# A hybrid Fourier, retention and attention transformer on one core: channel products between projection pairs, a new order on ScalarE, and an output projection begun early

## The chip, the cores and the metric

The kernel runs on one core of a Trainium2 chip. The metric is device time in microseconds, the median of the runs of one program. Engines work in order, each on its own list of instructions, and wait for each other through semaphores: TensorE (PE; its weight loads are shown as PEld), VectorE (DVE), ScalarE (ACT), GpSimd (POOL) and SyncE (SP), which issues the DMAs.

## What is computed

Two layers act on 512 latent tokens and 256 context tokens of width 1024. Each layer is a half-step gated feed-forward network, a token mixing, and another feed-forward network; inputs of each are normalized and modulated by a vector computed from a condition. The token mixing is where the change lies (cut from the reference):

```python
def fourier_mix(u):
    g = u.reshape(b, l, FOURIER_GROUPS, FOURIER_GROUP_DIM)
    y = jnp.fft.fft2(g, axes=(1, 3), norm='ortho').real

# retention, per head, chunks of 128 tokens, in both directions
intra_decay = where(causal, exp(diff * log_gamma), 0)
q_decay, k_decay = exp((pos + 1) * log_gamma), exp((cl - 1 - pos) * log_gamma)
scores = einsum(qc, kc) * intra_decay
kv = einsum(kc, k_decay, vc)      # state = state * chunk_decay + kv
out = scores @ vc + (qc @ state) * q_decay

# attention, 8 heads on 2 key/value heads, window of 128 and the context
m = maximum(s_loc.max(-1), s_ctx.max(-1), sink)
denom = exp(s_loc - m).sum(-1) + exp(s_ctx - m).sum(-1) + exp(sink - m)
o = (p_loc / denom) @ v_window + (p_ctx / denom) @ v_ctx

out = concatenate([y_f, y_ret, y_att], -1) @ w_o
```

In the second layer the context tokens give keys, values and states only.

## The kernel before, in words

Activations stand transposed: 128 channels on the partitions, tokens along the free axis, 8 blocks of channels. A float32 product of weights and activations is made as three products of rounded parts (high by high, high by low, low by high). The work is a list of phases. In each, a "unit" is 128 output channels for all tokens, accumulated over 8 or 11 blocks in one of two PSUM tiles `pg[0]`, `pg[1]` (two banks each); units go in pairs. `unit` (line 710) waits for split weights (`s_w`) and for the PSUM tile to be read (`s_free`), and calls `split_product` (line 703). SyncE loads weights into `raw`; ScalarE rounds them to `whi` (`split_hi`, line 1117), VectorE subtracts to `wlo` (`split_lo`, line 1445). A unit's weights are split while the other unit of the pair is multiplied.

The token mixing has three parts.

**Input projection** (`win`), 16 tiles of 128 channels: 0 and 1 Fourier, 2 to 5 retention queries and keys, 6 and 7 values, 8 and 9 gates, 10 to 13 attention queries, 14 keys, 15 values. TensorE runs the first pair apart and the other seven in hardware loops over pairs. ScalarE copies each finished unit to `z` (line 1409), VectorE rotates the tiles of queries and keys (lines 1911 to 1914).

**Mixing** (`mix`; one per engine, order written out by hand). TensorE's list is: wait until the projection's PSUM tiles are read and rotated; channel products (line 853: for each block of 128 tokens, both Fourier tiles by a table of cosines and sines, into one of two halves `pa[0]`, `pa[1]` of a PSUM tile), which ScalarE (even blocks, line 1269) and VectorE (odd blocks, line 1748) scale and copy into `pq`; sequence products of `pq` with the table `dft_sb` (lines 866, 870) into `pn` and then `pg[0]`; transposes of values and keys for the retention (lines 881, 884); chunk states (line 905); retention turns, one per block and pair of heads: scores (line 918), decay by VectorE (line 1742), values and cross part (lines 931, 933); the variance of the output (line 943); attention. Meanwhile ScalarE loads the table of exponentials (line 1265), makes the key decays, state decays and query decays (lines 1272 to 1275) and the exponential of the decay table (line 1278), and copies retention queries (line 1232); VectorE makes the arguments of the decay table (lines 1685, 1689) and decays the queries (line 1697). Low parts of the Fourier output are made by VectorE inside the retention turns (`y_low`, line 1662), after turn 2 and after turn 4 or 5. GpSimd copies states to `cross` (line 645), subtracts for the low parts of attention keys `ak_lo` and queries `aq_st` (line 633), and from step to step of the attention runs its own small list.

**Attention** goes over units q (48 in layer 0, 32 in layer 1; one is a block of 128 queries of one head), two units a pair `pr`. PSUM tile `pg[q % 2]` holds the scores. For unit q: TensorE scores (lines 962 to 968); VectorE the maximum (line 1808) and its negation with the sink, `negm` (line 1816); ScalarE the exponential `prob` (line 1325), with the row sum `den`; TensorE transposes (line 1006); VectorE and ScalarE copy them (`probT`, lines 1801, 1337); per pair TensorE multiplies by the values (line 1023). Beside this runs the denominator of each pair: GpSimd `esink = negm + sink` (line 671), ScalarE its exponential (line 1315), GpSimd the sum (line 675), VectorE the reciprocal (line 1813), GpSimd the spreading (line 689), TensorE a transpose (line 1030), ScalarE a copy `rden_t` (line 1342), VectorE the product with the values `oatt` (line 1826), ScalarE its high part (line 1347) and GpSimd its low part `xlo` (line 633), which counts `s_y` up. GpSimd also makes the low part of the next head's queries behind the sum of two of the pairs. All engines issue in the order of their loops over q; in ScalarE's, the order inside a step is sink exponential, `prob`, copy of transposes, copy of reciprocals, high part, next queries.

**Output projection** (`wo`), 8 units of 8 blocks (0, 1 Fourier, 2, 3 retention, 4 to 7 one head of each key/value group): TensorE first waits until `s_y` has counted all low parts, then multiplies. It is the last phase of the mixing; the second feed-forward network follows.

## Time and profile before

| | before |
|---|---|
| time, median of 3 runs | 2759.57 us (2758.16 to 2765.77) |
| profiled execution | 2770.8 us |
| its span | 2769.0 us |
| mean granted TensorE clock | 0.985 of full |
| TensorE (PE) busy | 2684.2 us, 97% |
| weight loads (PEld) busy | 2300.5 us, 83% |
| VectorE busy | 1520.8 us, 55% |
| ScalarE busy | 691.9 us, 25% |
| GpSimd busy | 94.8 us, 3% |
| DMA | 316.89 MB, mean 114 GB/s |

A row of a timeline gives the start and the length in us, the engine, the line and the operation, how many (x), and in brackets the idle time of the engine before it and what ended that. Matmuls overlap in the pipeline, so the length of a group exceeds the time until the next one can start by the tail of its last matmul. "issue" in brackets stands for a wait whose releaser the profile does not name. The granted clock is a share of TensorE's 2.4 GHz: 1.00 is that level, 0.50 the other level of 1.2 GHz.

### The profile page before, as it was taken

The numbers are of one execution on the slowest core, as the hardware profiler recorded it, in microseconds if no ns is written. First come the engines' busy times: TensorE is split into PE (matmuls) and PEld (weight loads), VectorE is DVE, ScalarE is ACT, GpSimd is POOL, SyncE is SP. The second block draws the span as 40 slices with busy tenths as digits, with TensorE's granted clock in tenths as the row PEclk, the third lists the DMA queues.
The fourth block names the chain that finished last, engine by engine and source line by source line (L and its number), as shares of the span: only waits on it lengthen the run. The fifth ranks groups of instructions, "written<-read, shape, count | busy, mean of one in ns | idle before, by whom it ended". The sixth has DMA issues, their size and how long they took to land.

```text
span 2769.0 us, 42294 instructions
## 1 busy us (share of the span) xinstructions
PE 2684.2 (97%) x15515; PEld 2300.5 (83%) x15515; DVE 1520.8 (55%) x2621; ACT 691.9 (25%) x1075; POOL 94.8 (3%) x211
## 2 busy tenths in 40 slices
PE   6999999999988999999999999999999988999998
PEld 4888888888867878888888888888887867888887
DVE  5776477544366377625773677347535465533343
ACT  4111111132256231111111311111123245422222
POOL 0000000000033000000000000000000022000000
PEclk8999999999989999999999999999999999999999
DMA  7877477412200167626762577257522200233332
GB/s 230 197 183 176 116 184 185 114 51 84 61 1 1 46 148 185 163 59 161 185 169 60 123 185 176 65 142 185 130 65 84 76 16 7 80 96 106 91 100 90
DMA packets 485790, 316.89 MB, mean 114 GB/s; under 512 B 30588, under 2 KB 483664, under 8 KB 485712
## 3 DMA queue, kind: packets, MB, share of 16 engines
q1 hardware_dynamic: 485712, 315.88, 44.7%
q8 instruction: 46, 0.75, 0.1%
q14 instruction: 32, 0.26, 0.0%
HBM read 313.73 MB, written 2.10 MB: 114 GB/s over the span
## 4 chain that ended last, share of the span: by engine, by line
PE 90%; DVE 4%; ACT 2%; issue 2%; POOL 1%; DMA 0%; SPq 0%; POOLq 0%; DVEq 0%; ACTq 0%
PE pg L703 79%; PE pg L770 5%; PE p L718 1%; PE pn L1006 1%; DVE mx L1808 1%; PE pg L962 1%; DVE xlo L1592 1%; ACT whi L1117 1%; DVE probT L1801 1%; DVE tnorm L1584 1%; ACT prob L1325 0%; DVE wlo L1445 0%; PE p L1023 0%; PE pg L967 0%; POOL ak_lo L633 0%
## 5 line engine op out<-in xcount | busy, mean ns | idle before, releaser
L703 PE MATMUL pg<-xhi,whi 128*128 128x512 f32 x2880 | 803.5, 347 | 5.7 <-POOL xlo L633 3.7
L703 PE MATMUL pg<-xhi,wlo 128*128 128x512 f32 x2880 | 796.5, 345 | 0.0
L703 PE MATMUL pg<-xlo,whi 128*128 128x512 f32 x2880 | 796.0, 345 | 0.0
L1117 ACT CAST whi<-raw 128x1024 fp32r<-128x1024 f32 (+1 forms) x288 | 321.8, 1118 | 1075.1 <-PE pg L703 1066.4
L1445 DVE TENSOR_TENSOR wlo<-raw,whi 128x1024 fp32r<-128x1024 f32 (+1 forms) x288 | 377.7, 1312 | 351.8 <-ACT whi L1117 349.2
L703 PEld LDWEIGHTS pg<-xhi,whi 128*128 128x128 f32 x2880 | 455.4, 188 | 74.4 <-issue 4.0
L703 PEld LDWEIGHTS pg<-xlo,whi 128*128 128x128 f32 x2880 | 456.1, 188 | 71.2
L703 PEld LDWEIGHTS pg<-xhi,wlo 128*128 128x128 f32 x2880 | 455.0, 188 | 70.3
L1529 DVE SCALAR_TENSOR_TENSOR part<-ada,cond,part 128x256 f32<-128x256 f32 x960 | 465.2, 485 | 32.7
L1655 DVE SCALAR_TENSOR_TENSOR h<-pg,gcol,h 128x512 f32 (+1 forms) x118 | 71.4, 639 | 456.8 <-PE pg L703 456.8
L703 PE MATMUL pg<-ahi,whi 128*128 128x512 f32 x1100 | 307.4, 347 | 0.0
L703 PE MATMUL pg<-alo,whi 128*128 128x512 f32 x1100 | 304.6, 345 | 0.0
L703 PE MATMUL pg<-ahi,wlo 128*128 128x512 f32 x1100 | 304.6, 345 | 0.0
L1372 ACT ACTIVATE gate<-pg 128x768 f32<-128x768 f32 (+1 forms) x88 | 66.8, 759 | 575.5 <-PE pg L703 574.4
L703 PEld LDWEIGHTS pg<-alo,whi 128*128 128x128 f32 x1100 | 174.9, 188 | 28.3
L703 PEld LDWEIGHTS pg<-ahi,wlo 128*128 128x128 f32 x1100 | 173.3, 188 | 27.1
L703 PEld LDWEIGHTS pg<-ahi,whi 128*128 128x128 f32 x1100 | 174.1, 188 | 26.0
L1851 DVE TENSOR_TENSOR gate<-gate,pg 128x768 f32<-128x768 f32 (+1 forms) x88 | 78.1, 887 | 137.7 <-PE pg L703 137.7
L770 PE MATMUL pg<-xhi,whi 128*128 128x256 f32 (+1 forms) x240 | 86.3, 359 | 7.8 <-DVE xlo L1592 4.3
L1856 DVE TENSOR_TENSOR alo<-gate,ahi 128x768 f32 (+3 forms) x88 | 78.5, 892 | 9.7
L770 PE MATMUL pg<-xlo,whi 128*128 128x256 f32 (+1 forms) x240 | 81.8, 341 | 0.0
L770 PE MATMUL pg<-xhi,wlo 128*128 128x256 f32 (+1 forms) x240 | 81.5, 339 | 0.0
(206 smaller groups left out, 1966.8 us busy)
## 6 DMA issues: line engine op xcount, KB each, us to landing
ada<-in_w_ada SPq DMA_DIRECT2D x512, 256.0 KB, 4.2
raw<-in_ffn_w_in SPq DMA_DIRECT2D x176, 512.0 KB, 3.9
raw<-in_ffn_w_out SPq DMA_DIRECT2D x64, 704.0 KB, 4.5
raw<-in_w_in SPq DMA_DIRECT2D x24, 512.0 KB, 3.9
ada_first<-in_w_ada SPq DMA_DIRECT2D x8, 1024.0 KB, 12.1
raw<-in_w_in SPq DMA_DIRECT2D x16, 256.0 KB, 3.4
raw<-in_w_o SPq DMA_DIRECT2D x16, 256.0 KB, 2.7
raw<-in_w_o SPq DMA_DIRECT2D x32, 128.0 KB, 2.9
```

Source lines behind the costliest of these rows:

```text
L703: last = nc.tensor.matmul(pg[s][:, p0:p1], w[:, s, k], v[:, k, p0:p1], start=(k == 0 and n == 0), stop=(k == kt - 1 and n == 2))
L718: last = nc.tensor.matmul(pa[1][:, 2 * b:2 * b + 2], part[:, b * P:(b + 1) * P], halves, start=True, stop=True)
L770: last = nc.tensor.matmul(pg[s][:, c0:c0 + p1 - p0], w[:, s, k], v[:, k, p0:p1], start=(k == 0 and n == 0), stop=(k == kt - 1 and n == 2))
L962: nc.tensor.matmul(pg[q % 2][:, c0:SEQ], w, k[s][:, lo * P:(lo + nk) * P], start=first_, stop=False, skip_group_check=True)
L1006: last = nc.tensor.transpose(pn[:, dst:dst + P], prob[:, q % 2, j * P:(j + 1) * P], ident)
L1117: nc.scalar.copy(whi[:, s, 0:nk], raw[:, s, 0:nk]).then_inc(s_whi[s], 1)
L1372: nc.scalar.activation(gate[:, 0:t], pg[0][:, 0:t], ACT.Silu).then_inc(s_free[0], 1)
L1445: nc.vector.tensor_sub(wlo[:, s, 0:nk], raw[:, s, 0:nk], whi[:, s, 0:nk].bitcast(f32)).then_inc(s_w[s], 1)
L1529: ins = nc.vector.scalar_tensor_tensor(part[:, :], ada[q][:, a], cond2[:, n:n + 1], part[:, :], ALU.mult, ALU.add)
L1655: last = nc.vector.scalar_tensor_tensor(hv, pg[s][:, p0:p1], gcol[:, col, v:v + 1].rearrange("p o v -> p (o v)"), hv, ALU.mult, ALU.add)
L1851: nc.vector.tensor_tensor(gate[:, 0:t], gate[:, 0:t], pg[1][:, 0:t], ALU.mult).then_inc(s_free[1], 1)
L1856: nc.vector.tensor_sub(lo, gate[:, 0:t], hi.bitcast(f32)).then_inc(s_a[m, hf], 1)
```

## The change

The channel products, their copies and everything for the decays move into the input projection; `pq` becomes six tiles of which three lie behind the rotation tables and three behind `dft_sb`. On TensorE `mix` begins with the sequence products; of the waits for the projection's PSUM tiles each stands now where its tile is needed. The loops of the projection are cut at pairs 4, 5 and 6. `y_low` moves from the retention turns to attention steps 4 and 6. In ScalarE's attention loop the sink exponential goes behind `prob`, and the copy of the reciprocals goes from step 2pr + 4 to 2pr + 5; `negm` gets 8 columns for this. `first_out` begins the output projection: blocks 0 to 3 and then 4 to 6 of unit 0 stand at the end of TensorE's attention loop, behind the last values and behind the last transpose of reciprocals; block 7 waits for all low parts. The core of the diff:

```diff
-        pq = place("pq", [P, TOK // P, 4 * P], f32, m0)
+        pq = [place(f"pq{tt}", [P, 4 * P], f32, (m0 + 6144, t0 + 2 * (SEQ // P) * HALF_F * 4)[tt // 3] + tt % 3 * 2048)
+              for tt in range(TOK // P)]
...
-        negm = sb("negm", [P, 4])
+        negm = sb("negm", [P, 8])
...
+        def channel_pairs(l):
+
+            return {4 + tt // 2: (tt, tt + 1) for tt in range(0, win_tokens(l, F_T) // P, 2)}
...
-                        nc.gpsimd.tensor_tensor(esink[:, p], negm[:, p], sink[:, hd:hd + GROUP + 1:GROUP], ALU.add
+                        nm = slice(pr % 4 * 2, pr % 4 * 2 + 2)
...
-                for s in range(2):
-                    pe.wait_ge(s_free[s], read_value(i, WIN_TILES // 2 - 1))
-                pe.wait_ge(s_zr[l], len(ROPE_TILES))
-
-                for tt in range(nt):
+            def channel_dft(l, tiles):
+
+                for tt in tiles:
                     if tt >= 2:
                         pe.wait_ge(s_pq[l][tt % 2], tt // 2)
...
+            def first_out(i, k0, k1):
+
+                l, t = phases[i][1], tokens(i)
+                if k0 == 0:
+                    pe.wait_ge(s_w[0], pair0(i) + 1)
+                    pe.wait_ge(s_free[0], read_value(i, -1))
+                pe.wait_ge(s_y[l], y_count(l) - (0 if k1 == KD else pair_units(l) // 2))
+                for k in range(k0, k1):
+                    for n, (w, v) in enumerate(((whi, xhi), (whi, xlo), (wlo, xhi))):
+                        for p0, p1 in [(0, SEQ)] + ([(SEQ, TOK)] if t == TOK else []):
+                            last = nc.tensor.matmul(pg[0][:, p0:p1], w[:, 0, k], v[:, k, p0:p1],
+                                                    start=(k == 0 and n == 0), stop=(k == KD - 1 and n == 2))
+                if k1 == KD:
+                    last.then_inc(s_unit[0], 1)
+
...
                 for b in range(2):
                     pe.wait_ge(s_pq[l][b], nt // 2)
                 pe.wait_ge(s_dft[l], 16)
                 for ft in range(2):
                     dst = (pn, pg[0])[ft]
+                    if ft:
+                        pe.wait_ge(s_free[0], read_value(i, WIN_TILES // 2 - 1))
                     for tt in range(nt):
                         for cs in range(2):
-                            w = pq[:, tt, ft * 256 + cs * P:ft * 256 + cs * P + P]
+                            w = pq[tt][:, ft * 256 + cs * P:ft * 256 + cs * P + P]
...
+                pe.wait_ge(s_free[1], read_value(i, WIN_TILES // 2 - 1))
+                pe.wait_ge(s_zr[l], len(ROPE_TILES))
...
+                    if q == len(units) + 1:
+                        first_out(i + 1, 0, 4)
+                    if q == len(units) + 2:
+                        first_out(i + 1, 4, KD - 1)
...
-                        with pe.Fori(b, e) as j:
-                            unit(i, 0, j, xhi, xlo, tw)
-                            unit(i, 1, j, xhi, xlo, tw)
+                        while b < e:
+                            c = min(e, 4) if b < 4 else b + 1 if b < 6 else e
+                            if c - b == 1:
+                                unit(i, 0, b, xhi, xlo, tw)
+                                unit(i, 1, b, xhi, xlo, tw)
+                            else:
+                                with pe.Fori(b, c) as j:
+                                    unit(i, 0, j, xhi, xlo, tw)
+                                    unit(i, 1, j, xhi, xlo, tw)
+                            if c in channel_pairs(l):
+                                channel_dft(l, channel_pairs(l)[c])
+                            b = c
...
-                    pe.wait_ge(s_y[l], y_count(l))
-                    with pe.Fori(0, units // 2 - 1) as j:
+                    first_out(i, KD - 1, KD)
+                    unit(i, 1, 0, xhi, xlo, t)
+                    with pe.Fori(1, units // 2 - 1) as j:
...
+            def channel_copy(l, tt):
+
+                act.wait_ge(s_f1, f1_count(l, tt))
+                length = SEQ if tt < SEQ // P else CTX
+                nc.scalar.mul(pq[tt][:, :], pa[0], float((length * HD) ** -0.5)).then_inc(s_pq[l][0], 1)
+
+            def decay_exps(l):
+
+                act.wait_ge(s_da, l + 1)
+                for dr in range(2):
+                    b = (2 * l + dr) * RH
+                    nc.scalar.activation(kdec[:, :, dr], lg[:, b:b + RH], ACT.Exp, scale=kpos[:, dr:dr + 1])
+                nc.scalar.activation(sdk[:, :], lgq[:, l], ACT.Exp, scale=float(P)).then_inc(s_kd, 1)
+                for hd in range(RH):
+                    nc.scalar.activation(qdt[:, hd], qpos, ACT.Exp, scale=lgq[:, l, hd:hd + 1])
+                nc.scalar.activation(dec[:, :, :], dec[:, :, :], ACT.Exp).then_inc(s_de, 1)
 
             def norm(i, m):
...
-                nc.scalar.preload_act_table_set("natural_log_exp_and_others")
-                for tt in range(0, nt, 2):
-                    act.wait_ge(s_f1, f1_count(l, tt))
-                    length = SEQ if tt < SEQ // P else CTX
-                    nc.scalar.mul(pq[:, tt], pa[0], float((length * HD) ** -0.5)).then_inc(s_pq[l][0], 1)
-                for dr in range(2):
-                    b = (2 * l + dr) * RH
-                    nc.scalar.activation(kdec[:, :, dr], lg[:, b:b + RH], ACT.Exp, scale=kpos[:, dr:dr + 1])
-                nc.scalar.activation(sdk[:, :], lgq[:, l], ACT.Exp, scale=float(P)).then_inc(s_kd, 1)
-                for hd in range(RH):
-                    nc.scalar.activation(qdt[:, hd], qpos, ACT.Exp, scale=lgq[:, l, hd:hd + 1])
                 query_copies(0)
-                act.wait_ge(s_da, l + 1)
-                nc.scalar.activation(dec[:, :, :], dec[:, :, :], ACT.Exp).then_inc(s_de, 1)
                 def sine_copy(ft):
...
-                    if q >= 2 and q % 2 == 0 and q <= len(units):
-                        pr = (q - 2) // 2
-                        p = slice(pr % 2 * 2, pr % 2 * 2 + 2)
-                        act.wait_ge(s_es, pair_count(l, pr))
-                        nc.scalar.activation(esink[:, p], esink[:, p], ACT.Exp).then_inc(s_ee, 1)
...
-                        b = slice(q % 4, q % 4 + 1)
+                        b, nm = slice(q % 4, q % 4 + 1), slice(q % 8, q % 8 + 1)
                         nc.scalar.activation(prob[:, q % 2, 0:w], pg[q % 2][:, TOK - w:TOK], ACT.Exp,
-                                             bias=negm[:, b], accum_out=den[:, b]).then_inc(s_p[l], 1)
+                                             bias=negm[:, nm], accum_out=den[:, b]).then_inc(s_p[l], 1)
+                    if q >= 2 and q % 2 == 0 and q <= len(units):
+                        pr = (q - 2) // 2
+                        p = slice(pr % 2 * 2, pr % 2 * 2 + 2)
+                        act.wait_ge(s_es, pair_count(l, pr))
+                        nc.scalar.activation(esink[:, p], esink[:, p], ACT.Exp).then_inc(s_ee, 1)
...
-                    if q >= 4 and q % 2 == 0 and q < len(units) + 3:
-                        pr = (q - 4) // 2
+                    if q >= 5 and q % 2:
+                        pr = (q - 5) // 2
...
+                        if n == AQ_T:
+                            nc.scalar.preload_act_table_set("natural_log_exp_and_others")
...
+                        if n % 2 and (n + 1) // 2 in channel_pairs(l):
+                            channel_copy(l, channel_pairs(l)[(n + 1) // 2][0])
+                        if n == 13:
+                            decay_exps(l)
...
+            def channel_copy(l, tt):
+
+                dve.wait_ge(s_f1, f1_count(l, tt))
+                length = SEQ if tt < SEQ // P else CTX
+                nc.vector.tensor_scalar(pq[tt][:, :], pa[1], float((length * HD) ** -0.5), None, ALU.mult
+                                        ).then_inc(s_pq[l][1], 1)
+
+            def decay_args(l):
+
+                for hd in range(RH):
+                    b = (2 * l + 1) * RH + hd
+                    done = mark(nc.vector.tensor_scalar(dec[:, hd], dist_sb[:, :], nlg[:, b:b + 1], None, ALU.mult))
+                dve.wait_ge(s_dv, done)
+                for hd in range(RH):
+                    b = 2 * l * RH + hd
+                    last = nc.vector.scalar_tensor_tensor(dec[:, hd], dist_sb[:, :], lg[:, b:b + 1], dec[:, hd],
+                                                          ALU.mult, ALU.min)
+                last.then_inc(s_da, 1)
+
...
-                    if r in (2, 5 if nt > 4 else 4):
-                        k = 0 if r == 2 else 1
-                        y_low(l, k, ysum[k][:, 0:tq], 0, tq, k + 1)
...
-                        nc.vector.tensor_scalar(negm[:, b], mx[:, b], sink[:, hd:hd + 1], -1.0, ALU.max, ALU.mult
+                        nm = slice((q + 1) % 8, (q + 1) % 8 + 1)
+                        nc.vector.tensor_scalar(negm[:, nm], mx[:, b], sink[:, hd:hd + 1], -1.0, ALU.max, ALU.mult
                                                 ).then_inc(s_nm[l], 1)
...
+                    if q in (4, 6):
+                        k = (q - 4) // 2
+                        y_low(l, k, ysum[k][:, 0:tq], 0, tq, k + 1)
...
+                        if n % 2 and (n + 1) // 2 in channel_pairs(l):
+                            channel_copy(l, channel_pairs(l)[(n + 1) // 2][1])
+                        if n == 8:
+                            decay_args(l)
...
```

## Rows read from the trace of the kernel before

**Rows 1.** The page, section 4: the chain that ended last, shares by engine.

```profile
PE 90%; DVE 4%; ACT 2%; issue 2%; POOL 1%; DMA 0%; SPq 0%; POOLq 0%; DVEq 0%; ACTq 0%
```

**Rows 2.** By stretch: length; busy of PE, PEld, DVE, ACT, POOL; granted clock; DMA.

```profile
785.70:795.70 10.00, 10.00 (x54) 6.10 (x52) 3.29 (x5) 0.81 (x1) 8.08 (x5) 0.50 0.01 2
812.50:820.00 7.50, 6.08 (x36) 5.42 (x37) 3.31 (x9) 3.54 (x11) 3.87 (x7) 0.54 0.00 0
903.70:912.20 8.50, 8.50 (x40) 7.36 (x41) 0.00 (x0) 0.00 (x0) 0.00 (x0) 0.80 0.01 2
2340.70:2349.20 8.50, 8.45 (x30) 6.85 (x31) 0.75 (x2) 1.05 (x1) 0.00 (x0) 0.80 0.01 2
```

**Rows 3.** Timeline of TensorE, end of the projection and Fourier stage, both layers.

```profile
750.96 0.51 PE L703 MATMUL pg<-xhi,wlo 128*128 128x512 f32 x2
752.42 1.97 PE L853 MATMUL p<-consts,z 128*128 128x256 f32 x8 [0.95 <-issue]
...
759.95 3.71 PE L866 MATMUL pn<-dft_sb,pq 128*128 128x257 f32 x16 [0.83 <-issue]
...
2221.30 0.52 PE L703 MATMUL pg<-xhi,wlo 128*128 128x512 f32 x2
...
2228.39 3.71 PE L866 MATMUL pn<-dft_sb,pq 128*128 128x257 f32 x16 [0.83 <-issue]
```

**Rows 4.** Timeline of the retention, layer 0, and attention's first scores, both layers.

```profile
781.68 8.64 POOL L633 TENSOR_TENSOR ak_lo<-z,ak_hi 64x768 fp32r<-64x768 f32 x4
781.70 2.60 DVE L1662 TENSOR_TENSOR xlo<-ysum,xhi 128x768 fp32r<-128x768 f32 x1
...
784.69 0.49 PE L918 MATMUL pg<-z 64*128 64x128 f32 x4 [1.76 <-DVE sdec L1742]
...
790.40 3.67 POOL L633 TENSOR_TENSOR aq_st<-z,aq_st 64x768 fp32r<-64x768 f32 x2
...
799.72 0.39 PE L962 MATMUL pg<-ak_hi,aq_st 128*128 128x256 f32 x1 [0.20 <-DVE osq L1762]
...
2259.22 0.36 PE L962 MATMUL pg<-ak_hi,aq_st 128*128 128x256 f32 x1 [2.22 <-POOL aq_st L633]
```

**Rows 5.** Timeline of the attention, layer 0: one pair, and VectorE at step 5.

```profile
816.67 0.56 DVE L1801 COPY probT<-pn 128x384 f32<-128x384 f32 x1 [2.42 <-PE pn L1006]
...
886.48 0.21 DVE L1816 TENSOR_SCALAR negm<-mx,sink 128x1 f32<-128x1 f32 x1
...
887.05 0.20 ACT L1315 ACTIVATE esink<-esink 128x2 f32<-128x2 f32 x1 [0.94 <-POOL esink L671]
...
887.16 0.78 ACT L1325 ACTIVATE prob<-pg,negm 128x640 f32<-128x640 f32 x1
...
888.09 0.39 PE L962 MATMUL pg<-ak_hi,aq_st 128*128 128x256 f32 x1 [0.39 <-ACT prob L1325]
...
890.71 0.15 DVE L1813 RECIPROCAL rden<-rden 128x2 f32<-128x2 f32 x1
```

**Rows 6.** TensorE's waits: 800:820, 820:902, 2259:2277, 2277:2341 (us in total, times, longest).

```profile
PE pg L962 <- ACT prob L1325: 3.1, 2, 2.2
...
PE pg L962 <- ACT prob L1325: 7.9, 20, 0.6
...
PE pg L962 <- ACT prob L1325: 3.0, 2, 1.9
...
PE pg L962 <- POOL aq_st L633: 3.0, 3, 1.3
PE pg L962 <- ACT prob L1325: 2.8, 9, 0.4
```

**Rows 7.** Timeline of TensorE, end of attention and output projection, both layers.

```profile
900.94 0.66 PE L1023 MATMUL p<-probT,vatt 128*64 128x128 f32 x8 [0.32 <-ACT probT L1337]
...
903.69 0.59 PE L703 MATMUL pg<-xhi,whi 128*128 128x512 f32 x2 [1.83 <-POOL xlo L633]
...
2340.75 0.47 PE L703 MATMUL pg<-xhi,whi 128*128 128x512 f32 x1 [1.85 <-POOL xlo L633]
```

## What the change will do to the time, predicted before it ran

> **What bounds the kernel now.** I read the chain of waits first: TensorE holds 90% of it [rows 1]. So only time in which TensorE waits, or runs at half clock, can be won. The stages outside the token mixing repeat one matrix product without a gap; the change touches none of them, so what a mixing stage saves arrives at the end. Then I went through the two mixing stages in order of time and looked for three things: gaps of TensorE, what ended them, and stretches with a low granted clock. There are four such places per layer: the Fourier stage between the input projection and the two-dimensional transform's second half, the retention, the attention, and the start of the output projection. In several of them the granted clock falls to half after TensorE has waited [rows 2].
>
> The sum goes against the profiled execution's own 2770.8 us (span 2769.0); the runs shown have a median of 2759.57, 11.2 less. I take the difference off the median.
>
> **Fourier stage.** Before, TensorE ends the projection at 750.96 + 0.51 = 751.47 and starts the sequence transform at 759.95, 8.48 us later; in layer 1 it is 2221.30 + 0.52 = 2221.82 to 2228.39, 6.57 us [rows 3]. Between lie the channel products (24 and 16 matmul instructions) and waits for ScalarE's and VectorE's copies, which read and free two PSUM halves in turn. The change issues the products after projection pairs 3, 4 and 5 (3 and 4 in layer 1), where nothing waits for the copies: the next use of a half comes a pair later, some 17 us. The products themselves stay on TensorE. Eight of them take 1.97 us and sixteen of nearly the same width 3.71, so one more costs (3.71 - 1.97)/8 = 0.218 us: 5.2 us for 24 and 3.5 for 16 [rows 3]. Left are 8.48 - 5.2 = 3.3 and 6.57 - 3.5 = 3.1. From the first I take 0.2, since ScalarE ends its last weight split only after the projection and its query copies, formerly level with the transform, now trail it a little: 3.1 + 3.1 = **6.2 us**. Bounds: -2.6, if each of the 40 costs the duration of a single one, 1.97 - 7 x 0.218 = 0.44 (17.6 us instead of 8.7), and 6.6 with nothing taken off and 0.1 more a layer. The decay arithmetic on VectorE, the exponentials on ScalarE and the table load cost nothing: these two engines are idle for most of the projection, as weights are split for the next pair while TensorE works on this one. Were that cover gone, TensorE would wait for split weights after tiles 8 and 13, by at most the moved work there, about 2 us on each engine (an estimate: some ten small instructions each). No DMA issue moves; SyncE's order is unchanged.
>
> **Retention.** VectorE's low-part subtraction of the Fourier output (line 1662) leaves this stage. In layer 0 it took 2.60 us at 781.70, VectorE's next decay product came late, and TensorE waited 1.76 us at 784.69. Then the clock was 0.50 for 10 us [rows 2, 4]. What TensorE did in that stretch would take 5 us at full clock; I take 4.2 as won, since with VectorE's product between two score products a turn cannot halve. With 1.8 for the wait: 6.0 us. The limit is GpSimd: keys and queries are ready at 790.40 + 3.67 = 794.07, and attention started at 799.72, so 5.6 could be won, and up to 1.4 more because the four key subtractions took 8.64 us, partly beside line 1662 [rows 4]. In layer 1 TensorE waits 2.22 us for GpSimd [rows 4]: nothing is won there. **6.0 us**, bounds 1.8 (the clock falls anyway) and 7.0.
>
> The subtraction goes to attention steps 4 and 6. Its 2.60 us began 0.02 us after a GpSimd operation [rows 4]. The Trainium skill (SBUF — State Buffer, "Who interferes with whom") says a VectorE operation with two SBUF inputs and a GpSimd operation that reads SBUF exclude each other for a whole instruction. By that rule, against this move, a query split of GpSimd can hold the moved subtraction as well; the row agrees with it, and by the rule alone the sum would lose up to one split a layer. I charge nothing: VectorE waits 2.4 us for transposes after step 4 [rows 5], and about as long after step 6, so the subtraction moves into that idle time; a split takes 3.67/2 = 1.8 us [rows 4], and if nothing hid it, that is the price a layer.
>
> **Attention.** For one pair of units: VectorE's negated maximum ends at 886.48 + 0.21 = 886.69, but ScalarE's probability exponential starts at 887.16, because the sink exponential ahead of it on ScalarE waited 0.94 us for GpSimd; TensorE's next scores wait 0.39 us for it [rows 5]. The change puts the sink exponential behind, and the copy of the reciprocals a step later. So about 0.45 us a pair, in 18 pairs after 820 us, is 8.1; TensorE's own waits there sum to 7.9 us [rows 5, 6]. I take 7.0, since VectorE's chain of transpose copy, maximum and negation is late next. Before 820 us one wait is 2.2 us [rows 6], half of which a free exponential gives back: 1.1; and of 7.5 us at clock 0.54 (3.4 lost [rows 2]) I take 1.0. Layer 1: 2.8 us of such waits [rows 6], all taken; 0.9 of its first long wait of 1.9 and 0.6 of clock. Against it: TensorE waits three times, 3.0 us, for GpSimd's next queries [rows 6], which come behind the denominator, and that comes behind the sink exponential. This one is now behind a probability exponential of 0.8 + 0.1: 0.6 later three times, -1.7. Attention: 7.0 + 2.1 + 2.8 + 1.5 - 1.7 = **11.7 us**; bounds 0 and 20.
>
> **Output projection.** Before, its first product waits for the last head's low part: the last values end at 900.94 + 0.66 = 901.60 and it starts at 903.69; layer 1 has a wait of 1.85 and 0.25 before it [rows 7]. Seven eighths of the first unit no longer need that head: they start when the values are done. Half a unit (4.2 us, 2.8 in layer 1) is in front of the last transpose of reciprocals; the steps behind this transpose took about 2 us before, and three more blocks (3.2 or 2.1 us) cover them. So 2.1 us a layer. Then 8.5 us had clock 0.80 in each layer [rows 2], 1.7 lost; without the wait I expect none. 2 x 3.8 = **7.6 us**; bounds 2 and 7.6.
>
> Sum: 6.2 + 6.0 + 11.7 + 7.6 = 31.5 us. 2770.8 - 31.5 = 2739.3, and against the median 2759.57 - 31.5 = 2728.1. About 0.3% (8 us) is what a measurement can tell from no change.
>
> **Rivals.**
> *The denominator comes too late (slower).* VectorE's reciprocal stands ahead of its negated maximum. If the sink exponential, now behind a probability exponential, made it late, every one of 40 pairs would pay that exponential and its gap, 0.78 + 0.1 = 0.88 us: 35.2 us, with attention's 11.7 gone: 2759.6 - 19.8 + 35.2 = 2775.0. It decides once the delay passes the slack: the sink exponential ended at 887.25 and the reciprocal started at 890.71, over 3 us later [rows 5]. Strongly against it: 3%.
> *Attention is bound otherwise.* VectorE's chain takes the place of ScalarE's waits and 11.7 us are not won: 2739.8. For it: after a transpose VectorE needs copy, maximum and negation one behind the other; against: ScalarE ends most waits [rows 6]. 15%.
> *The clock does not come back.* TensorE still waits for GpSimd before attention and is as idle by shares as before; 4.2 + 1.6 + 3.4 = 9.2 us are lost: 2737.3. 14%.
> *More is won.* The rows of waits leave out the tail of the matmul before each wait; with 0.44 - 0.22 = 0.2 us for each of 33 waits [rows 6] and 1.4 us more of clock it is 8 us more: 2720.1. 15%.
> *The move gives nothing.* The products cost 0.44 each in the projection (8.9 us more), attention is bound otherwise and the clock stays: 31.5 - 8.9 - 11.7 - 9.2 = 1.7 us won, 2757.9. 3%.
> My forecast has 50%.
>
> **The numbers.** Range 2715 to 2743: it takes in attention bound otherwise and the clock, with 3 us for the scatter of a median, and the gain of more; the first and last rival and the far ends of sums of bounds stay outside. Faster by over 0.3%: all but two rivals, 94%; within 0.3%: 3%; slower: 3%.
>
> **What would show it.** Right: the sequence transform starts within 0.1 us of the projection's end; eight channel products in about 1.8 us three times inside layer 0's projection, two in layer 1's; no wait over 0.6 us in layer 0's retention and a clock of 1.00 from 780 to 792; attention in layer 0 under 93 us against 101.8 before; TensorE's waits for probabilities below 4 us; output projection without a wait and with clock 1.00 in its first 8 us. In layer 1 the three waits for GpSimd's queries remain and grow. Wrong: a reciprocal that waits for the denominator, a weight wait in the projection, or clock 0.50 in the same places.

## The result, and the profile of the changed kernel

The changed kernel takes 2738.89 us (median of 4 runs, 2738.31 to 2743.11), the kernel before 2762.67 (2758.16 to 2766.2): a ratio of 0.9918 (95% interval 0.9897 to 0.9939). Beside later experiments the same two stood at 2741.47 and 2762.96, 0.9924 (0.9910 to 0.9937). So 21 to 24 us are won; 31.5 were forecast. Faster was right and the range (2715 to 2743) holds the time, but the sum was a third to a half too large. Between the two profiled executions, though, the gain is 2770.8 - 2739.1 = 31.7 us, just the sum. That is the puzzle of this case.

What was to be seen if the steps were right. First TensorE's timeline: the products inside the projection, the end of it, and a wait in layer 1.

```profile
683.92 1.89 PE L853 MATMUL p<-consts,z 128*128 128x256 f32 x8
685.46 0.69 PE L709 MATMUL pg<-xhi,whi 128*128 128x512 f32 x2
...
2149.25 1.89 PE L853 MATMUL p<-consts,z 128*128 128x256 f32 x8
...
2175.30 0.50 PE L709 MATMUL pg<-xhi,whi 128*128 128x512 f32 x1 [0.63 <-DVE wlo L1493]
...
2202.91 0.53 PE L709 MATMUL pg<-xhi,wlo 128*128 128x512 f32 x2
2203.27 3.63 PE L887 MATMUL pn<-dft_sb,pq 128*128 128x257 f32 x16
```

Eight products take 1.89 us, the next unit starts 1.54 us after their start, and the transform follows the projection at once, where it was 8.48 and 6.57 us late [rows 3]. The weight wait of 0.63 us was on the list of things that would be wrong.

The same engine at the attention's start in both layers and at the output projection, which now begins with the early unit (line 867):

```profile
790.00 0.38 PE L986 MATMUL pg<-ak_hi,aq_st 128*128 128x256 f32 x1 [0.20 <-DVE osq L1811]
...
883.44 0.66 PE L1047 MATMUL p<-probT,vatt 128*64 128x128 f32 x8 [0.32 <-DVE probT L1847]
884.02 0.62 PE L867 MATMUL pg<-xhi,whi 128*128 128x512 f32 x2
...
2233.38 0.36 PE L986 MATMUL pg<-ak_hi,aq_st 128*128 128x256 f32 x1 [2.71 <-POOL aq_st L638]
```

The wait of 1.83 us ahead of the output projection [rows 7] is gone; GpSimd's wait in layer 1 is longer than before (2.22 [rows 4]).

The granted clock (the number ahead of the last two) in stretches that answer to those of before [rows 2]:

```profile
780.00:790.00 10.00, 9.80 (x105) 6.51 (x105) 4.26 (x9) 2.71 (x4) 9.20 (x6) 1.00 0.01 2
810.00:820.00 10.00, 8.26 (x79) 6.63 (x76) 8.09 (x25) 6.09 (x27) 4.01 (x13) 1.00 0.01 2
884.00:892.00 8.00, 8.00 (x48) 6.98 (x47) 1.12 (x4) 0.86 (x3) 1.19 (x3) 1.00 0.01 3
```

These are all at full clock, as forecast. Last, the waits over the whole program (us in total, times, longest), ScalarE's and then TensorE's:

```profile
ACT prob L1362 <- DVE negm L1863: 47.5, 61, 3.9
```

TensorE:

```profile
PE pg L986 <- ACT prob L1362: 8.9, 11, 2.3
PE pg L986 <- POOL aq_st L638: 5.9, 3, 2.7
PE pn L1030 <- DVE probT L1847: 4.6, 12, 0.8
```

Before, ScalarE's probability exponential waited 10.3 us in 12 places for VectorE's negation. The sink exponential is no longer in its way, and now it is VectorE that is late. TensorE's waits for the probabilities went from 16.8 us to 8.9; the forecast named under 4, and under 93 us for layer 0's attention, which takes 94.1 (next table). Both signs fell short.

To see where the time goes I cut each profiled execution at the same events: ScalarE's first projection output (z), the first sequence transform, the first attention scores, the end of the last values, VectorE's first residual addition of the output projection, and the end of the span. Differences of start times, in us; the names of the other kernels are explained with the experiments.

```
columns: layer 0: z to transform, transform to attention, attention, its end to the first addition;
         between the layers; layer 1: the same four; from there to the end
before          130.52  39.77  101.88  12.51  1210.16   104.12  30.83   79.41   9.71   420.66
before again    130.52  34.89  100.74  12.51  1209.35   104.08  30.83   79.11   8.07   420.78
changed         126.42  33.69   94.10   8.98  1208.42   101.77  30.11   75.50   6.13   422.19
changed again   127.06  33.67   94.06   8.91  1211.33   101.82  30.10   77.23   6.08   422.85
m_fourier       128.29  33.41   94.23   8.98  1206.53   104.14  30.16   75.51   6.09   422.12
m_ylow          126.42  35.19   93.23   8.97  1210.77   101.80  30.76   74.87   6.13   422.66
m_act           126.43  33.69  100.76   8.99  1211.44   101.80  30.12   79.24   6.08   422.43
m_sink          126.42  33.69  100.18   8.91  1208.63   101.81  30.11   78.65   6.08   422.27
m_out           126.42  33.69   94.09  11.08  1212.82   101.81  30.12   77.21   8.03   420.80
m_actout        126.43  33.69  101.44  12.48  1206.63   101.83  30.08   80.45   9.53   420.76
v_quiet         126.42  33.67   92.43   8.97  1209.20   101.78  30.09   75.76   6.09   422.32
v_wfin          127.06  33.69   94.21   8.99  1209.34   101.82  30.08   76.57   6.12   420.31
v_all           126.43  33.70   92.45   8.99  1206.98   101.81  27.95   75.22   6.11   420.39
```

### The profile page after: what moved, and what is told of

Read it like the earlier page. It is cut to its first block, busy times and chain, and to the rows that moved or that the text cites. A ratio compares the mean times of both kernels' runs of the same rounds, so it can differ in the third digit from the quotient of the medians.

```text
span 2737.2 us, 42267 instructions
## 1 busy us (share of the span) xinstructions
PE 2664.7 (97%) x15515; PEld 2290.5 (84%) x15515; DVE 1521.2 (56%) x2621; ACT 692.3 (25%) x1075; POOL 93.7 (3%) x211
## 4 chain that ended last, share of the span: by engine, by line
PE 91%; DVE 4%; ACT 2%; issue 1%; POOL 1%; DMA 0%; SPq 0%; DVEq 0%; ACTq 0%; POOLq 0%
PE pg L709 79%; PE pg L776 4%; PE p L1047 1%; PE pn L1030 1%; PE pg L986 1%; PE p L724 1%; DVE xlo L1640 1%; DVE tnorm L1632 1%; PE pg L867 1%; ACT whi L1155 0%; DVE wlo L1493 0%; PE pg L991 0%; DVE probT L1847 0%; DVE mx L1854 0%; ACT xhi L1244 0%
## 5 line engine op out<-in xcount | busy, mean ns | idle before, releaser
L709 PE MATMUL pg<-xhi,whi 128*128 128x512 f32 (+1 forms) x2856 | 794.5, 347 | 4.1 <-DVE wlo L1493 4.0
L709 PE MATMUL pg<-xhi,wlo 128*128 128x512 f32 (+1 forms) x2856 | 788.6, 344 | 0.0
L709 PE MATMUL pg<-xlo,whi 128*128 128x512 f32 (+1 forms) x2856 | 787.1, 344 | 0.0
L709 PEld LDWEIGHTS pg<-xlo,whi 128*128 128x128 f32 x2856 | 450.4, 188 | 69.3
```

What stands on the lines that cost most here:

```text
L709: last = nc.tensor.matmul(pg[s][:, p0:p1], w[:, s, k], v[:, k, p0:p1], start=(k == 0 and n == 0), stop=(k == kt - 1 and n == 2))
```

## Experiments

**One part taken back at a time.** Four kernels made from the changed one; the kernel before stood at 2764.42 beside them. The changed kernel was not run beside these four, and the kernel before stood 1.5 to 1.8 us lower beside it, so a difference to the changed kernel's two medians may be too large by about 2 us.

*m_fourier*: the Fourier move undone, with the copies, the decay arithmetic and the table load.

```diff
-                            if c in channel_pairs(l):
-                                channel_dft(l, channel_pairs(l)[c])
...
+                channel_dft(l, range(nt))
```

> The changed kernel with one part taken back: the channel products, their copies, the decay arithmetic, the exponentials and the table load stand again behind the projection, in the order of the kernel before. By the forecast this part is worth 6.2 us, so this kernel stands 6.2 us above the changed one (2745.1 against a median of 2738.9): the sequence transform begins 8.5 and 6.6 us after the projection's end, and everything behind it is shifted by as much. By the rival that the products cost more inside the projection than behind it, it stands less than 2 us above. The trace of the changed kernel lets me expect slightly more than the forecast in layer 0, 3.6 to 4.1 us.

Measured: 2746.17 us (0.9933 of the kernel before, 0.9922 to 0.9945), so worth 4.7 to 7.3 us by the medians, which takes in the forecast's 6.2. In layer 0 its stage is only 1.87 us longer than the changed kernel's, against 4.10 for the kernel before. That is not the products: this execution ran the 14 full projection units with 8.32 us from one to the next where the others have 8.48 (see the last section), and 14 x 0.16 = 2.2 us make up the difference. The gap itself is back, 8.48 us.

*m_ylow*: the subtraction of line 1710 back in the retention turns.

```diff
-                    if q in (4, 6):
...
+                    if r in (2, 5 if nt > 4 else 4):
```

> The changed kernel with the two low-part subtractions of the Fourier output back in the retention turns. The forecast's account: 6.0 us lost in layer 0's retention and nothing won in the attention, so 2744.9. The rival account, from the changed kernel's trace: in the attention each subtraction runs beside a GpSimd query split and delays VectorE's next maximum, so taking them out of it gives back some 1 us each in four places; then this kernel stands only 2 to 3 us above the changed one, with attention of layer 0 about 2 us shorter than 94.1 us, and the wait of VectorE's decay product and the clock of 0.50 are back at 780 to 792 us. A third account: the low clock in the retention was an accident of one execution; then the clock there is 1.00 and the loss is below 2.5 us.

Measured: 2739.14 us (0.9911, 0.9898 to 0.9923). Nothing is lost at all. TensorE's wait is back, the low clock is not (780 to 800 us at 1.00):

```profile
777.25 8.88 POOL L638 TENSOR_TENSOR ak_lo<-z,ak_hi 64x768 fp32r<-64x768 f32 x4
777.26 0.95 DVE L1710 TENSOR_TENSOR xlo<-ysum,xhi 128x768 fp32r<-128x768 f32 x1
...
780.50 2.08 DVE L1710 TENSOR_TENSOR xlo<-ysum,xhi 128x768 fp32r<-128x768 f32 x1
...
782.97 0.49 PE L942 MATMUL pg<-z 64*128 64x128 f32 x4 [1.25 <-DVE sdec L1797]
```

The retention is 1.5 us longer in layer 0 and 0.65 in layer 1, the attention 0.87 and 0.63 shorter. The forecast's 6.0 is refuted. The rival account (a collision in the attention) is right in kind but not in size: it named 2 us in layer 0 and had the low clock come back. The third holds: the low clock was no fixture of this place.

*m_act*: ScalarE's old order in the attention, the copy of the reciprocals with it. *m_sink*: the sink exponential alone (run later, expected below), whose edit is shown.

```diff
+                    if q >= 2 and q % 2 == 0 and q <= len(units):
+                        ... sink exponential of the pair ...
                     if q < len(units):
                         ... probability exponential ...
-                    if q >= 2 and q % 2 == 0 and q <= len(units):
-                        ... sink exponential of the pair ...
```

> The changed kernel with ScalarE's old order in the attention: the sink exponential ahead of the probability exponential, the copy of the reciprocals at even steps. The forecast gives this order 11.7 us, so 2750.6. The rival, that VectorE's maximum and negation are late next whatever ScalarE does, gives 0 to 5 us: 2739 to 2744. Both are told apart by the length of layer 0's attention: 101.8 us (as before) by the forecast, 94 to 97 by the rival.

Measured: 2752.44 us (0.9955, 0.9943 to 0.9967). Layer 0's attention takes 100.76 us, 6.7 more; layer 1's 79.24, 2.0 to 3.7 more. So the order is worth 8.7 to 10.4 us by the traces, and by the medians 11 to 13.5: nearer to the forecast's 11.7 than to the rival's 0 to 5.

> The changed kernel with the sink exponential alone back ahead of the probability exponential; the copy of the reciprocals stays at odd steps. The forecast put almost all of the order's 11.7 us on the sink exponential: then layer 0's attention takes 100 to 101 us, as with the whole old order (100.8), and this kernel stands 11 to 13 us above the changed one. If the copy of the reciprocals carries half of it, layer 0's attention takes 97 us and the kernel stands about 6 us above.

Measured: 2752.66 us (0.9963, 0.9949 to 0.9977), layer 0's attention 100.18. This kernel stands 11.2 us above the changed one, run beside it (2741.47). By one trace of each, the sink exponential carries 6.1 of the 6.7 us, the reciprocals' copy 0.6.

*m_out*: the output projection waits again for the last head.

```diff
-                    first_out(i, KD - 1, KD)
-                    unit(i, 1, 0, xhi, xlo, t)
-                    with pe.Fori(1, units // 2 - 1) as j:
+                    pe.wait_ge(s_y[l], y_count(l))
+                    with pe.Fori(0, units // 2 - 1) as j:
```

> The changed kernel without the early start of the output projection: TensorE again waits for the low part of the last head before its first product. The forecast gives this part 2 x (2.1 of wait + 1.7 of clock) = 7.6 us, so 2746.5, with a wait of 1.8 us and a clock near 0.80 in the first 8.5 us of each output projection. The rival, that the low clock there was owed to the long half-busy attention of the kernel before and not to this wait, gives 2 x 2.1 = 4.2 us: 2743.1, with a clock of 1.00.

Measured: 2746.93 us (0.9931, 0.9918 to 0.9943). The wait is back, the low clock is not:

```profile
881.77 0.66 PE L1047 MATMUL p<-probT,vatt 128*64 128x128 f32 x8 [0.32 <-DVE probT L1842]
...
884.51 0.59 PE L709 MATMUL pg<-xhi,whi 128*128 128x512 f32 x2 [1.82 <-POOL xlo L638]
...
886.00 0.51 PE L709 MATMUL pg<-xlo,whi 128*128 128x512 f32 x2
```

2.1 us in layer 0 and 1.95 in layer 1, by the stage table: the rival's 4.2, less 1.4 to 2.1 that this kernel wins at the end of the program (below). The medians say 5.5 to 8.0 us. In the profiled execution what is missing lies between the layers (1212.8 us against 1208.4 and 1211.3) and in layer 1's attention, 77.21 us, which has two falls of the clock as in the changed kernel's second trace (77.23; what the second fall costs is worked out below). Whether that is chance or comes with the edit, one trace can't tell; it stays open.

**Is the low clock a property of the place?** The same two kernels were profiled again.

> The kernel before, unchanged, profiled a second time. By the forecast its clock of 0.50 to 0.80 at 785 to 796, 812 to 820, 903 to 912 and 2340 to 2349 us belongs to the waits ahead of these places and is there again in all four. By the rival the chip's clock falls after low activity at places that differ from one execution to the next: then at least one of the four shows 1.00 and another place shows a fall in its stead. The first profiled execution took 2770.8 us; the runs without it had a median near 2763, so I expect about 2763, with 8 us less lost to the clock.

Measured: 2763.64 us (8 runs), the profiled execution with a span of 2758.3, 10.7 less than the first. By stretch, with the granted clock ahead of the last two numbers:

```profile
780.00:790.00 10.00, 8.64 (x90) 5.64 (x89) 5.42 (x9) 1.76 (x3) 9.70 (x5) 1.00 0.00 0
790.00:800.00 10.00, 8.88 (x67) 6.47 (x68) 7.50 (x14) 6.23 (x14) 3.27 (x4) 1.00 0.01 2
810.00:820.00 10.00, 9.22 (x87) 7.41 (x86) 6.00 (x23) 5.66 (x22) 4.58 (x12) 0.93 0.00 0
893.60:902.10 8.50, 6.67 (x29) 5.63 (x30) 1.08 (x3) 0.76 (x3) 1.09 (x3) 0.80 0.01 3
2331.50:2337.10 5.60, 5.57 (x25) 4.62 (x26) 0.00 (x0) 0.00 (x0) 0.00 (x0) 1.00 0.01 3
```

The retention and layer 1's output projection run at 1.00, where the first execution had 0.50 and 0.80 [rows 2]; layer 0's output projection has 0.80 again. Summed over stretches of 10 us, (1 - granted clock) x length is 41.1 us in the first execution of the kernel before, 22.8 in the second, and 22.8 and 26.1 in the two of the changed kernel. The first had a mean clock of 0.985; the 15 runs of the kernel before beside this one had 0.988 to 0.993 and at most 2769.15 us. So the profile under the forecast was an outlier, in its clock and in its time (2770.8 us).

The second execution differs in one thing more at that place. GpSimd's first key split and VectorE's subtraction start together, and now it is GpSimd that is held:

```profile
779.67 8.88 POOL L633 TENSOR_TENSOR ak_lo<-z,ak_hi 64x768 fp32r<-64x768 f32 x4
779.68 0.95 DVE L1662 TENSOR_TENSOR xlo<-ysum,xhi 128x768 fp32r<-128x768 f32 x1
```

In the first the subtraction took 2.60 us and the four splits 8.64 [rows 4]. TensorE's wait is 1.25 us here and was 1.76 there. Whether the longer wait brought the clock down in the first execution is not shown.

> The changed kernel, unchanged, timed beside the others and profiled a second time: median 2739 (2737 to 2743). The same question as for the kernel before: stretches of 1.00 stay at 1.00 if the clock follows the waits, and move if not. A second question: between identical matrix products of the projections and the feed-forward stages the pitch of one block of six matmuls is 1.04 us in some phases and 1.06 in others; if that belongs to the code, every phase repeats its pitch; if to the execution, the phases with 1.06 change.

Measured: 2741.47 us (0.9924, 0.9910 to 0.9937). A low clock at 950 to 970 us is there both times, one at 1520 to 1540 and one at 2090 only in the second. The pitch changes too, so it belongs to the execution (last section).

**Which wait brings the clock down at the output projection?**

*m_actout* = m_act's and m_out's edits together.

> The changed kernel with two parts taken back together: ScalarE's old order in the attention and the wait for the last head's low part ahead of the output projection. Alone, the first cost 6.7 us of attention in layer 0 and nothing in the output projection, the second 2.1 us of wait and no low clock. If the parts add up, the output projection of layer 0 begins as in the run without the early start (11.1 us to the end of its first unit, clock 1.00) and the kernel stands near 2741 + 13 + 7 = 2760. If the low clock of the kernel before (0.83, 12.5 us to the end of the first unit in both of its traces) needs both a slow attention and the wait, the unit ends after 12.5 us here.

Measured: 2755.93 us (12 runs, 0.9975, 0.9967 to 0.9984), with the first unit of the output projection as in layer 0 of the kernel before, 12.48 us:

```profile
890.67 0.33 PE L1054 MATMUL p<-consts,rden_b 128*128 128x128 f32 x1
892.82 0.59 PE L709 MATMUL pg<-xhi,whi 128*128 128x512 f32 x2 [1.82 <-POOL xlo L638]
893.24 0.51 PE L709 MATMUL pg<-xlo,whi 128*128 128x512 f32 x2
...
894.02 0.84 PE L709 MATMUL pg<-xhi,whi 128*128 128x512 f32 x2
```

And by stretch:

```profile
894.00:897.40 3.40, 3.40 (x13) 2.92 (x12) 0.00 (x0) 0.00 (x0) 0.00 (x0) 0.52 0.00 0
```

The rows of 0.84 in place of 0.51 us lie where the granted clock is 0.52. In layer 0 the fall came in all three profiled executions with the old order and the wait (two of the kernel before, one here), and in none of those with one of them alone (m_act, m_sink, m_out). In layer 1 it came in two of three (9.71, 8.07, 9.53). These six traces fit a fall that needs both, and layer 1 shows that even then it can fail to come. In layer 0 it costs 1.4 us (12.48 against m_out's 11.08), where TensorE is never idle.

Inside the attention the price depends on the place. In layer 0 it can be next to nothing: v_wfin has a fall at 800 to 810 us (0.83) and its attention takes 94.21 us against 94.10. In layer 1 it is not. The changed kernel, first and second execution:

```profile
2250.00:2260.00 10.00, 7.71 (x79) 6.80 (x77) 6.93 (x17) 5.94 (x20) 3.42 (x10) 1.00 0.00 2
```

```profile
2250.00:2260.00 10.00, 7.72 (x70) 6.68 (x66) 6.11 (x15) 4.34 (x16) 2.95 (x8) 0.83 0.00 2
```

From the ninth probability exponential of layer 1 to the thirteenth it is 8.40 us in the first (2255.28 to 2263.68) and 9.77 in the second; m_fourier, m_ylow and v_wfin, without a fall there, have 8.39 to 8.40, m_out with one has 9.70. So this fall costs 1.3 to 1.4 us, most of the 1.7 us between 75.50 and 77.23.

**The collision, and two things seen on the way.** In the changed kernel, at attention step 4 of layer 0 (VectorE and GpSimd):

```profile
803.78 1.80 POOL L638 TENSOR_TENSOR aq_st<-z,aq_st 64x768 fp32r<-64x768 f32 x1
...
804.43 1.96 DVE L1710 TENSOR_TENSOR xlo<-ysum,xhi 128x768 fp32r<-128x768 f32 x1
...
807.74 0.69 ACT L1362 ACTIVATE prob<-pg,negm 128x512 f32<-128x512 f32 x1 [1.88 <-DVE negm L1863]
```

GpSimd's split ends at 805.58; from there to VectorE's end at 806.39 are 0.81 us, about what the subtraction takes by itself. *v_quiet* moves the two subtractions to steps 8 and 10.

```diff
-                    if q in (4, 6):
-                        k = (q - 4) // 2
+                    if q in (8, 10):
+                        k = (q - 8) // 2
...
-                            dve.wait_ge(s_y[l], 4 + pr - 1)
+                            dve.wait_ge(s_y[l], 4 + pr - 1 - (q < 10))
```

> The changed kernel with the two low-part subtractions at attention steps 8 and 10, where GpSimd does no query split, in place of 4 and 6. If each of them is long because a GpSimd operation runs beside it (1.96 and 2.53 us in layer 0, 1.17 and 1.34 in layer 1), they now take 0.95 and 0.68 us, VectorE's next maximum comes earlier, and attention is shorter by 0.9 us in layer 0 and 0.6 in layer 1: 1.5 us in all. If the length comes from something else, the durations stay and the time is the same as the changed kernel's.

Measured: 2740.57 us (0.9920, 0.9907 to 0.9934), not to be told from the changed kernel's 2741.47. But the trace is clear:

```profile
810.74 0.95 DVE L1710 TENSOR_TENSOR xlo<-ysum,xhi 128x768 fp32r<-128x768 f32 x1
813.36 0.95 DVE L1710 TENSOR_TENSOR xlo<-ysum,xhi 128x768 fp32r<-128x768 f32 x1
...
2255.84 0.68 DVE L1710 TENSOR_TENSOR xlo<-ysum,xhi 128x512 fp32r<-128x512 f32 x1
2259.79 0.68 DVE L1710 TENSOR_TENSOR xlo<-ysum,xhi 128x512 fp32r<-128x512 f32 x1
```

Half the duration, and 1.67 us less attention in layer 0. Layer 1's attention is 75.76 us against 75.50 and 77.23, but its falls of the clock differ: v_quiet has one where the changed kernel's second execution has it. From the fifth exponential to the thirteenth v_all (below), with the same places for the subtractions and no fall there, takes 18.03 us against the changed kernel's 18.41: the gain in layer 1 is about 0.4 us, and in v_quiet the fall hides it.

The Trainium skill ("SBUF — State Buffer", "Who interferes with whom") says that a VectorE instruction with two SBUF inputs contends with a GpSimd instruction that reads SBUF, that only one of them can hold the shared port, and that the order of issue decides which one waits. The rows above agree. It works the other way round too: in m_ylow VectorE kept its 0.95 us, and GpSimd's four splits took 8.88 us in place of 7.46. There, as in both executions of the kernel before, the two start within 0.02 us of each other, GpSimd first by the trace, and once VectorE was held and twice GpSimd; which issued first can't be read at that distance.

The second thing: all traces with the early unit lose 1.4 to 2.1 us at the very end. In the changed kernel:

```profile
2722.45 0.35 SPq L623 DMA_DIRECT2D wfin<-in_final_norm_w  x1
...
2727.51 2.48 DVE L1982 SCALAR_TENSOR_TENSOR osb<-pg,fstat,wfin 128x1024 f32<-128x1024 f32 x2 [5.13 <-DMA wfin<-in_final_norm_w]
```

The DMA view of its last 16 us has, beside the data queue, one packet of the instruction queue (packets, MB, share):

```profile
q8 instruction: 1, 0.02, 0.5%
```

The output waits for the final norm's weight. It lands 4.9 to 5.6 us after its issue in the seven traces that have the early unit and this late issue, and each has such a packet beside the load; the packet's share rises from 0.4% in the trace with 4.9 us to 0.7% in that with 5.6. In the four without the early unit (both of the kernel before, m_out, m_actout) there is none in these 16 us, and the weight lands after 3.5 to 3.6 us:

```profile
2730.95 0.35 SPq L623 DMA_DIRECT2D wfin<-in_final_norm_w  x1
...
2734.54 2.48 DVE L1977 SCALAR_TENSOR_TENSOR osb<-pg,fstat,wfin 128x1024 f32<-128x1024 f32 x2 [3.66 <-DMA wfin<-in_final_norm_w]
```

(m_out's timeline.) *v_wfin* issues this transfer two pairs into the last phase.

```diff
+                        if i == len(phases) - 1 and a == 0:
+                            load_step(0, b, layer)
+                            load_step(1, b, layer)
+                            for s in range(2):
+                                sp.wait_ge(s_free[s], read_value(i, -1))
+                            sp.dma_start(wfin[:, :], final_norm_w.partition_broadcast(P)).then_inc(s_wf, 16)
+                            a = 2
...
-            sp.dma_start(wfin[:, :], final_norm_w.partition_broadcast(P)).then_inc(s_wf, 16)
```

> The changed kernel with one transfer earlier: the final norm's weight, which VectorE needs for the first output tile, is issued two pairs into the last phase in place of behind it. In the seven traces with the early first unit an instruction-queue packet runs beside this transfer and it lands 5.0 to 5.7 us after its issue; in the three without, it lands after 3.6 us. If the output waits for this transfer, the end comes 1.5 to 2.2 us earlier than in the changed kernel, and VectorE's first output operation waits for ScalarE's statistics; if something else ends it, the time is the same. Near 2739 against 2741 for the changed kernel on the same chip.

Measured: 2736.73 us (4 runs, 0.9905, 0.9890 to 0.9919). The load takes 5.05 us here too, beside the phase's other transfers and without such a packet, but nothing waits for it. VectorE now waits for ScalarE's statistics and the last stage takes 420.31 us, 1.9 to 2.5 less:

```profile
2725.28 1.28 DVE L1988 SCALAR_TENSOR_TENSOR osb<-pg,fstat,wfin 128x1024 f32<-128x1024 f32 x1 [3.02 <-ACT fstat L1479]
```

*v_all* = v_quiet + v_wfin + the splits, and ScalarE's high parts ahead of them, ordered by head:

```diff
                 for v in range(KV_HEADS):
+                    keys_low(v)
                     query_low(0, v)
...
+                    if q == 0:
+                        pe.wait_ge(s_ql[l], 1)
+                    elif q == 1:
+                        pe.wait_ge(s_kl[l], 2 * KV_HEADS)
+                        pe.wait_ge(s_ql[l], KV_HEADS)
```

> The changed kernel with three edits: the low-part subtractions at attention steps 8 and 10, the final norm's weight loaded earlier, and GpSimd's key and query splits ordered by head, so that the first scores need only the first head's three. In layer 1 the first scores waited 2.7 us for all six splits; now they start when the retention ends, and the second ones wait for what is left, so 1 to 1.5 us less from the start of the retention to the attention's end. Layer 0 shows no change there, since GpSimd was done in time. Sum against the changed kernel: 1.5 to 2.2 (last transfer) + 1.5 to 2.5 (subtractions) + 1 to 1.5 = 4 to 6 us, 2735 to 2737. If the pieces are lost in the scatter of clock and pitch, 2741 as the changed kernel.

Measured: 2733.04 us (4 runs, 2729.06 to 2734.09), 0.9893 of the kernel before (0.9879 to 0.9908). Its first two scores in layer 1:

```profile
2225.48 0.39 PE L999 MATMUL pg<-ak_hi,aq_st 128*128 128x256 f32 x1 [0.55 <-DVE osq L1823]
...
2227.53 0.35 PE L999 MATMUL pg<-ak_hi,aq_st 128*128 128x256 f32 x1 [1.21 <-POOL aq_st L644]
```

The first scores start 2.15 us sooner (27.95 against 30.10), layer 0's attention is 1.65 shorter and the end 1.8 to 2.5: 5.6 to 6.3 us without layer 1's attention, the upper end of what was expected. Its slowest run is 3.7 us faster than the fastest of the changed kernel (2737.83), which was not run beside it.

## Why the forecast was right in sign and too large in size

Against the second execution of the kernel before, the stages touched by the change give 22.6 us with the changed kernel's first profile (4.10 + 1.20 + 6.64 + 3.53 + 2.31 + 0.72 + 3.61 + 1.94 - 1.41) and 19.8 with its second; the medians say 23.8 and 21.5. Step by step:

- **Fourier stage, 6.2 forecast**: 3.5 to 4.1 in layer 0 and 2.3 in layer 1, about 6. The sum is right in part by luck, since two misses of opposite sign cancel: layer 0 gave 0.4 to 1.0 more than its 3.1, layer 1 0.8 less. In layer 1 the products were priced at 3.5 us and cost 6.57 - 2.3 = 4.3: 0.63 of it is the weight wait, the cover that was said to be there and that I had bounded at 2 us.
- **Retention, 6.0 forecast**: 1.2 in layer 0. This is the step that failed: "I take 4.2 as won" of the clock. The clock was at 1.00 there in the second execution of the kernel before and in m_ylow, both with the subtraction in place. The wait was 1.25 and not 1.76. Against the first execution this stage gained 6.08 us, the forecast's 6.0: the size was that execution's. Layer 1 gave 0.7 where nothing was forecast.
- **"I charge nothing" for the subtraction in the attention**: the price is 0.9 us in layer 0 against having none there (m_ylow), 0.6 in layer 1, and 1.67 in layer 0 and about 0.4 in layer 1 against a quiet place (v_quiet, v_all). In layer 0 the price that the forecast named and dropped, one split (1.8 us), was the better one. Taken together the move of the subtraction is worth nothing that can be measured.
- **Attention, 11.7 forecast**: 6.7 + 1.9 to 3.6 = 8.6 to 10.3, with the 1.5 of the subtraction taken off. Undone by itself (m_act) the order costs 6.7 + 2.0 to 3.7. The mechanism was right, and m_sink puts nine tenths of it on the sink exponential. "VectorE's chain is late next" was right as well. Of the 1.6 us of clock in it, 1.0 was again the first execution's: its layer 0 took 101.88 us and the second's, with less of a fall, 100.74. In layer 1 the clock decides between the 1.9 and the 3.6: a second fall in the changed kernel costs 1.3 to 1.4. The 1.7 charged for GpSimd's queries is too much: TensorE's waits for them in layer 1 went from 5.2 to 5.9 us, 0.5 of it ahead of the first scores.
- **Output projection, 7.6 forecast**: 3.55 + 1.95 = 5.5. Twice 2.1 of wait: right. Twice 1.7 of clock: 1.4 in layer 0, and in layer 1 only in some executions. It was put down to the wait, but by m_act, m_out and m_actout it takes ScalarE's old order and the wait together.
- **Not in the sum**: the end of the program, 1.4 to 2.1 us longer.

The clock terms of the sum were 4.2 + 1.6 + 3.4 = 9.2 us, and the rival without them said 2737.3, 1.6 from the first median and 4.2 from the second. It was given 14% and a wrong reason: the clock did come back, but in a usual execution most of it had never been away. The sum was made against an execution of 2770.8 us and taken off a median of 2759.57; the 11.2 us between them were noted and not asked about. For the larger part they were the clock that I then counted as won. Against that execution the four terms hold one by one: 6.5, 6.8, 11.7 and 7.1 us by the stage table, with 1.5 lost at the end. The forecast of 2728.1 is 10.8 us below the measured 2738.89, and some 3 of these come from the median of three runs, 2759.57: with more runs the kernel before stood at 2762.67 to 2764.42.

The rival "attention is bound otherwise" said 2739.8, still nearer to the first median, and fell all the same, since the attention did gain: the time alone does not tell these rivals apart. No reciprocal waits for the denominator either.

## What to carry to other kernels

When the profiled execution is slower than the median, first find out in which stretches, and leave what those show (here half clock after short waits) out of a gain that is taken off the median; a second profile of the unchanged kernel shows which of them come back. Before an operation with two SBUF inputs is moved on VectorE, look at what GpSimd does at the new place, not only whether VectorE is idle there. And a load that the last output needs belongs well ahead of the end.

## What was unexpected in the hardware

**Two pitches.** The same loop of matmuls runs at one of two speeds, 2% apart, at full granted clock, and mostly keeps it for a whole phase. TensorE's timeline of the kernel before at 1460 us, first execution:

```profile
1460.09 0.51 PE L703 MATMUL pg<-ahi,whi 128*128 128x512 f32 x2
...
1461.12 0.51 PE L703 MATMUL pg<-ahi,whi 128*128 128x512 f32 x2
```

The second execution, the same stretch:

```profile
1460.25 0.53 PE L703 MATMUL pg<-ahi,wlo 128*128 128x512 f32 x2
...
1461.31 0.53 PE L703 MATMUL pg<-ahi,wlo 128*128 128x512 f32 x2
```

The second row of each is the third one after the first, six matmuls later: 1.03 to 1.04 us in the first execution and 1.06 in the second. At 1750 to 1800 us it is the other way round (1.06 in the first execution, 1.04 in the second), and the changed kernel has 1.06 at 1150 to 1250 us in one and 1.04 in the other. Summed over all such blocks the excess over 1.04 is 3.5 to 11.5 us in the executions profiled here, so a difference of a few microseconds between two single traces can come from this alone. What sets it stays open; no run tried to.

**An instruction packet beside a transfer** goes with 1.4 to 2.1 us more for a load of 512 KB. That the one causes the other is not shown: the runs show only that they come together, in seven traces against four, the load landing later where the packet's share is larger, and that an earlier load takes it off the path.
